# x in four column pieces, norm weights loaded ahead of the weights, and the first h writes ahead of a cast

## What is computed

```
def rms_norm(x, g):
    x = x.astype(jnp.float32)
    return x * lax.rsqrt(jnp.mean(x * x, axis=-1, keepdims=True) + RMS_EPS) * g.astype(jnp.float32)
...
        h = rms_norm(x, norm1_g[l])
        proj = h @ w_in[l]
        p_rwkv, p_attn, p_pool, p_gate = proj[..., :o1], proj[..., o1:o2], proj[..., o2:o3], proj[..., o3:]
        ...
    x = x + jnp.sum(gates * branch, axis=2) @ w_out[l]
    h2 = rms_norm(x, norm2_g[l])
    x = x + jnp.square(jax.nn.relu(h2 @ w_ff1[l])) @ w_ff2[l]
```

## Time and profile before

| | us |
|---|---|
| median of three runs | 462.98 |
| the profiled execution | 462.71 |
| its span, first to last instruction | 460.9 |
| PE busy | 455.3 |
| DVE busy | 311.4 |
| ACT busy | 237.6 |
| POOL busy | 33.0 |

### The profile page before, as it was taken

One profiled execution on the slowest core, in us unless ns is written; L12 is line 12 of the kernel. 1 busy time (PEld: TensorE's weight loads), 2 busy tenths in 40 slices (PEclk: granted clock), 3 DMA queues, 4 the chain that ended last, 5 costly groups with the idle time before them and its releaser, 6 DMA issues.

```text
span 460.9 us, 8234 instructions
## 1 busy us (share of the span) xinstructions
PE 455.3 (99%) x3404; PEld 382.5 (83%) x3404; DVE 311.4 (68%) x437; ACT 237.6 (52%) x357; POOL 33.0 (7%) x41
## 2 busy tenths in 40 slices
PE   8999999999999999999999999999999999999997
PEld 4999988788977777878888888888888888888885
DVE  4767699675464766766678758766666666666662
ACT  6787563746665557566533537444444444444430
POOL 2002000022680001002000000000000000000000
PEclk9999999999999999999999999999999999999999
DMA  8696536433524434456656564656666666566602
GB/s 274 208 287 195 185 98 206 142 106 94 155 79 137 127 107 142 134 154 177 189 184 184 175 195 152 206 182 186 184 190 196 197 190 184 185 184 193 211 5 91
DMA packets 48692, 76.87 MB, mean 167 GB/s; under 512 B 2576, under 2 KB 28944, under 8 KB 48656
## 3 DMA queue, kind: packets, MB, share of 16 engines
q1 hardware_dynamic: 48656, 76.36, 53.9%
HBM read 75.30 MB, written 1.05 MB: 166 GB/s over the span
## 4 chain that ended last, share of the span: by engine, by line
PE 96%; DMA 1%; DVE 1%; ACT 1%; SPq 0%; issue 0%
PE bank L501 22%; PE bank L502 21%; PE bank L503 21%; PE bank L552 13%; PE bank L554 6%; DMA stage<-in_w_in 1%; PE bank L759 1%; PE bank L778 1%; PE bank L653 1%; PE bank L641 1%; DVE xs L1494 1%; PE bank L854 1%; PE bank L818 1%; PE bank L518 1%; PE bank L864 1%; PE bank L831 0%
## 5 line engine op out<-in xcount | busy, mean ns | idle before, releaser
L1166 DVE TENSOR_TENSOR w_lo<-stage,w_hi 128x1024 fp32r<-128x1024 f32 x138 | 167.6, 1223 | 88.9 <-ACT w_hi L925 88.8
L925 ACT CAST w_hi<-stage 128x1024 fp32r<-128x1024 f32 x138 | 144.3, 1053 | 128.7 <-PE bank L503 72.3
L552 PE MATMUL bank<-h_two,w_hi 128*128 128x512 f32 x256 | 91.2, 399 | 0.3 <-DVE h_two L1414 0.3
L554 PE MATMUL bank<-h_two,w_lo 128*128 128x256 f32 x256 | 71.9, 281 | 0.0
L501 PE MATMUL bank<-w_hi,h_two 128*128 128x512 f32 x144 | 59.8, 415 | 0.0
L552 PEld LDWEIGHTS bank<-h_two,w_hi 128*128 128x128 f32 x256 | 48.1, 188 | 12.3 <-issue 0.6
L501 PE MATMUL bank<-w_hi,r_hi 128*128 128x512 f32 x144 | 56.4, 392 | 0.0
L503 PE MATMUL bank<-w_hi,h_two 128*128 128x512 f32 x144 | 56.4, 392 | 0.0
L502 PE MATMUL bank<-w_lo,h_two 128*128 128x512 f32 x144 | 56.4, 391 | 0.0
L502 PE MATMUL bank<-w_lo,r_hi 128*128 128x512 f32 x144 | 56.2, 390 | 0.0
L503 PE MATMUL bank<-w_hi,r_lo 128*128 128x512 f32 x144 | 56.0, 389 | 0.0
(11 more groups left out here) (239 smaller groups left out, 629.7 us busy)
## 6 DMA issues: line engine op xcount, KB each, us to landing
stage<-in_w_ff SPq DMA_DIRECT2D x64, 512.0 KB, 3.7
stage<-in_w_in SPq DMA_DIRECT2D x54, 512.0 KB, 4.3
stage<-in_w_branch SPq DMA_DIRECT2D x12, 512.0 KB, 4.5
stage<-in_w_out SPq DMA_DIRECT2D x8, 512.0 KB, 4.3
xs<-in_x SPq DMA_DIRECT2D x2, 512.0 KB, 3.9
out<-xs SPq DMA_DIRECT2D x4, 256.0 KB, 2.1
cst<-in_consts SPq DMA_DIRECT2D x1, 608.0 KB, 5.9
att<-in_w SPq DMA_DIRECT2D x1, 256.0 KB, 6.2
```

Of the source, the lines that this page charges most:

```text
L552: pe.matmul(o[:].rearrange("p (s t) -> p s t", s=2), wh[:, kk, cols], h_two[:, :, k], start=k == 0, stop=False)
L554: ins = pe.matmul(o[:, T:2 * T], wl[:, kk, cols], h_hi[:, k], start=False, stop=k == KD - 1)
L925: nc.scalar.copy(w_hi[:, v % RING], stage[:, v % STAGES]).then_inc(hi_done, 1)
L1166: dve.tensor_tensor(w_lo[:, v % RING], stage[:, v % STAGES], w_hi[:, v % RING].bitcast(F32), ALU.subtract)\
```

## The change

x is loaded in four transfers of 128 tokens by 512 columns, each with its own semaphore. The transfer of the vectors moves ahead of weight piece 0. ACT squares each piece by itself, scaled so that the sums are already divided by 1024, into four columns of `ss1` at a new place. DVE adds the two sums of a token tile and epsilon in one instruction. On ACT the first pair of `h_hi` writes stands ahead of `high(0)`, which follows before the second pair.

```diff
-        ss1, rs1, ss2, r2 = (small[:, 20 + 2 * i:22 + 2 * i] for i in range(4))
+        rs1, ss2, r2 = (small[:, 22 + 2 * i:24 + 2 * i] for i in range(3))
+        ss1 = small[:, 28:32]
...
-        x_in = [sem(f"x_in{tt}") for tt in range(TT)]
+        x_in = [sem(f"x_in{i}") for i in range(2 * TT)]
...
             for tt in range(TT):
-                sp.dma_start(xs[:, tt], x[0, P * tt:P * tt + P, :]).then_inc(x_in[tt], 16)
+                for h in range(2):
+                    w = slice(512 * h, 512 * h + 512)
+                    sp.dma_start(xs[:, tt, w], x[0, P * tt:P * tt + P, w]).then_inc(x_in[2 * tt + h], 16)
             sp.dma_start(cst[:, C_ID:C_ID + P], consts[:, C_ID:C_ID + P]).then_inc(id_in, 16)
+            sp.dma_start(vec[:], vecs).then_inc(vec_in, 16)
             for v in range(PIECES):
                 if v >= STAGES:
                     sp.wait_ge(lo_done, v - STAGES + 1)
                 sp.dma_start(piece_view(stage, v, STAGES), piece_dram(v)).then_inc(loaded[v % STAGES], 16)
-                if v == 0:
-                    sp.dma_start(vec[:], vecs).then_inc(vec_in, 16)
...
             for tt in range(TT):
-                act.wait_ge(x_in[tt], 16)
-                nc.scalar.activation(xn[:, tt], xs[:, tt], ACT.Square, accum_out=ss1[:, tt:tt + 1]).then_inc(ss_ready, 1)
-            high(0)
+                for h in range(2):
+                    act.wait_ge(x_in[2 * tt + h], 16)
+                    w = slice(512 * h, 512 * h + 512)
+                    nc.scalar.activation(xn[:, tt, w], xs[:, tt, w], ACT.Square, scale=D ** -0.5,
+                                         accum_out=ss1[:, 2 * tt + h:2 * tt + h + 1]).then_inc(ss_ready, 1)
             act.wait_ge(vec_in, 16)
             for i in range(4):
+                if i == 1:
+                    high(0)
                 o = take(act, ("x", i))
...
             for tt in range(TT):
-                dve.wait_ge(ss_ready, tt + 1)
-                dve.tensor_scalar(rs1[:, tt:tt + 1], ss1[:, tt:tt + 1], 1.0 / D, RMS_EPS, ALU.mult, ALU.add)\
-                   .then_inc(ms_ready, 1)
+                dve.wait_ge(ss_ready, 2 * tt + 2)
+                dve.scalar_tensor_tensor(out=rs1[:, tt:tt + 1], in0=ss1[:, 2 * tt:2 * tt + 1], scalar=RMS_EPS,
+                                         in1=ss1[:, 2 * tt + 1:2 * tt + 2], op0=ALU.add, op1=ALU.add).then_inc(ms_ready, 1)
```

## The result

The changed kernel takes 464.50 us, the median of five runs (464.28 to 464.95), against 462.87 for the kernel before in five runs (462.43 to 463.65). The ratio is 1.0035, 95% interval 1.0018 to 1.0052: 1.63 us slower, where 1.34 had been forecast. The profiled execution took 464.28 us, with a span of 462.5 against 460.9.

A forecast was written before the change was run, and what follows sets the result against it. PE was taken to bound the kernel, its dense stretch starting with unit 1. Unit 1 moving from 16.13 to 17.47 adds 1.34 to the 462.98 median: 464.3 us, range 463.2 to 465.2.

The forecast's parts named there:

- the x part: Front of the kernel: x in pieces makes DVE's multiply 0.3 to 0.4 us earlier, covered by PE's warm-up; worth nothing.
- the landing of piece 0: First weight load, issued later: lands between 8.15 and 9.6 us, 8.8 taken; harmless up to 9.65.
- the signs that the prediction had named for being right: New profile: first h_hi pair at 8.9 to 9.0, cast at 9.6 to 9.7 although piece 0 landed before, unit 1 about 17.5.
- What bounds: PE is dense from about 16 us on; any delay of unit 1, at 16.13 before, is paid in full at the end.
- The order on ACT: Cast of piece 0 put behind h_hi(0): cast 1.47 us later, unit 1 later by 1.34 us through DVE's low(2).
- The hand-over: Passing a result from DVE to PE takes 0.10 us, leaving DVE's chain 0.10 to 0.13 us of slack.
- A: PE's clock rises 1 us sooner in most executions, so x's 0.4 us becomes real: 463.9 us; chance 0.12.
- B: Piece 0 lands at 9.65 or later in both kernels: not slower, 462.9; chance 0.14 with what lies toward the forecast.
- C: Piece 0 lands after 9.65 in the new kernel only, each microsecond beyond added: 465.1 at 10.4; chance 0.07.
- D: PE's clock falls to 1.2 GHz in the longer gap ahead of the first unit: 466.1 us; chance 0.03.

The follow-up runs named there:

- the second measurement: The changed kernel, unaltered, measured and profiled again: 464.61 us against 462.74 for the kernel before, ratio 1.0036.

## Why the prediction was right, step by step

464.50 came where 464.3 had been forecast, and the chain of waits was the forecast one: the cast of piece 0 behind h_hi(0), and through it DVE's low(2) and unit 1. Two of the sum's smaller terms were mis-sized, the x part and the landing of piece 0. So two of the signs that the prediction had named for being right were missed in the first profile: the first h_hi pair stood at 9.23 instead of 8.9 to 9.0, and piece 0 had not landed well before the cast. With the order alone changed they come out (8.88, and piece 0 there at 8.0).

**What bounds.** Right. PE has no wait of some length after unit 1 began, in the changed kernel as before, and 1.62 us at 17.75 became 1.63 in the medians. Nothing was given back later.

**The order on ACT.** Right, and the main part: 1.34 forecast for it by itself, 1.23 measured, with the instants within 0.1 us.

**The x part.** Its sum failed. The step said that the last Square would begin at about 5.5, that the multiply would be 0.3 to 0.4 us earlier, and that PE's warm-up would cover this. The last Square began at 6.55, the multiply at 8.15 instead of 7.81, and PE waited 0.38 us for it after the eighth transpose. In place of nothing, the part cost 0.29 us at h_hi(0) (9.23 against 8.94). That is the 0.3 by which the changed kernel is slower than the forecast. The step took the landing of the second half for that of the last piece. Nothing in the profile backed this; all the parts of x in it had rows of 4 KB.

**The landing of piece 0.** The bound failed: 8.15 to 9.6 was given, 8.8 taken, and 9.98, 9.75 and 9.5 came in the three profiles with pieces and early norm weights. It left the result as it was, because ACT reached the cast no sooner: 9.96 in the first profile, 10.28 in the second. That is luck. Had x been in time in the first profile, ACT would have been free at 9.65, and piece 0 at 9.98 would have set the cast: two errors of the sum, each of 0.3, lay on top of each other and counted once. The Trainium skill, "DMA: Bandwidth & Descriptors", section "Bandwidth", speaks for large transfers. No run here shows that the size is what counts: with x in pieces piece 0 did land later (8.5 and 8.9 against 8.0 to 8.2, norm weights behind it in both), but it was also issued 0.94 later, and x was as late in two transfers of 512 KB with 2 KB rows as in four of 256 KB.

**The hand-over.** 0.10 was taken from DVE to PE; 0.05 came (17.70 to 17.75). So the slack that absorbed part of DVE's 1.80 was 0.18, not 0.10 to 0.13: 1.80 - 0.18 = 1.62.

**The rivals.** A: the clock rose earlier in the first profile of the changed kernel (the transposes began at 7.27 instead of 7.59), but x was then late and nothing was gained. B: with the loads of before, piece 0 landed at 8.0 to 8.15 in three profiles, and the order alone cost 1.23 us in the median of 12 executions, where B allows no loss; it fell. C: its condition came true, piece 0 after 9.65 in the pieces, in the first profile (9.98) and with the cast first (9.75). Its price did not, because x was late as well.

D, given 0.03, was too low as an event and too dear in price. It is what the run with the cast first shows at 11.70. In the changed kernel one of the five executions of the result (464.95) and four of the ten of the second measurement have a mean granted clock of 0.995 or 0.996; those four take 464.9 to 465.2 against 464.4 to 464.7 for the rest. The price is about 0.5, not the 1.8 of the sum. An estimate for it: the stretch at 0.50 cost 1.6 us in the run with the cast first (16 matmuls from 11.70 to 15.20 instead of 1.9 us), and PE has 0.9 us to spare in the changed kernel, since 48 matmuls at 0.12 from 11.09 would end at 16.85 and unit 1 waits for low(2) until 17.75; 0.7 is left. No trace of such an execution of the changed kernel was taken, so this is argued. The kernel before has such executions too, two of the 80 measured on the three chips, at 465.7 and 465.8; what happens in them isn't seen.

**The parts together.** Order + 1.23, pieces + 0.58, norm weights - 0.34 make + 1.47; the whole is + 1.63 and, in the second measurement, + 1.87 (+ 1.66 without the executions of low mean clock). Of the three parts only the first is clear of noise, so the sum is no proof. The traces say why the parts need not add: the gain of the norm weights needs the cast to stand first, and what the pieces cost depends on whether the cast waits for the load or for h_hi(0).

## What to carry to other kernels

On an engine that runs in order, an operation moved ahead of another takes its wait along. Before moving it, compare when its inputs are there with when those of the displaced one are: here 8.94 against 8.15, and the 0.71 us of the moved work came on top. Look also at the second engine in the chain. PE's own start moved by 0.98 us, but it was VectorE, with a slack of under 0.2 us behind the displaced cast, that set the end.

## What the runs showed of the hardware

- A 1 MB input in rows of 2 KB was complete between 6.1 and 6.9 us (four transfers, five profiles: the last Square stands at 6.13, 6.34, 6.55, 6.60 and 6.87; two transfers, one profile: 6.54), in rows of 4 KB at 5.4 to 5.6. In blocks of 64 partitions with 4 KB rows it was complete at 7.85.
- A transfer issued later can land earlier. With 30 KB of short rows ahead of piece 0, and piece 0 issued 0.5 us later for it, piece 0 landed at 7.3 to 8.2 in four profiles, against 8.0 to 8.2 in three with these rows behind it. With x in pieces the same move went with a later landing, 9.5 to 10.0 against 8.5 and 8.9. No run here tells why.
- TensorE's granted clock fell to 0.50, its 1.2 GHz level, in two profiles. With the cast first it fell at 11.7, after the transposes and 2.1 us of idleness, and was 1.00 again at 15.1; 16 matmuls of the first unit took 3.5 us instead of 1.9. With x in two column halves it fell at 10.3, 2.5 us after the warm-up had ended and with nothing between, and was 1.00 again at 13.8; 16 transposes took 3.5 us instead of 1.9. In the two profiles of the changed kernel, with gaps of 0.4 and 1.3 us and of 0.8 and 1.3 us around the second eight transposes, it stayed at 1.00.
- The granted clock of the profile reads 1.00 from 3 to 6 us of the kernel before too, where the weight loads stand 0.85 us apart instead of 0.44. So a granted 1.00 is no proof of full pace by itself; the distance between instructions is.
